# Byte offsets of the weight, activation and feed-forward buffers in a two-layer float32 kernel

## The reference

```
def swiglu(x, w_gate, w_up, w_down):
    return (jax.nn.silu(x @ w_gate) * (x @ w_up)) @ w_down
```

## Time and profile before

| what | before |
|---|---|
| median of 3 runs | 1321.93 us (1321.92 to 1321.98) |
| the profiled execution | 1321.68 us, of which the span of the trace is 1319.9 us |
| PE busy | 1308.6 us, 99% of the span, 7751 matmuls |
| PEld busy | 1105.4 us, 84% |
| DVE, ACT, POOL busy | 1079.1 us (82%), 713.6 us (54%), 205.1 us (16%) |
| share of PE in the chain of work that ended last | 97% |
| granted TensorE clock | 0.999 of full |

### The profile page before, as it was taken

One profiled execution on the slowest core, in us unless ns is written; L12 is line 12 of the kernel. 1 busy time (PEld: TensorE's weight loads), 2 busy tenths in 40 slices (PEclk: granted clock), 3 DMA queues, 4 the chain that ended last, 5 costly groups with the idle time before them and its releaser, 6 DMA issues.

```text
span 1319.9 us, 20183 instructions
## 1 busy us (share of the span) xinstructions
PE 1308.6 (99%) x7751; PEld 1105.4 (84%) x7751; DVE 1079.1 (82%) x1592; ACT 713.6 (54%) x840; POOL 205.1 (16%) x193
## 2 busy tenths in 40 slices
PE   9999999999999999999999999999999999999998
PEld 7888888888888888888899988888888888888886
DVE  6977788868999789998786999769777767878587
ACT  6444455665444454444465688854444466558553
POOL 2400001102000010000000035200000001654940
PEclk9999999999999999999999999999999999999999
DMA  8655556528577654876544565475655555654541
GB/s 274 223 191 191 191 179 204 191 77 306 192 260 267 242 186 146 269 233 222 184 160 155 175 215 180 145 257 166 210 194 196 197 171 160 200 172 143 175 152 56
DMA packets 158445, 254.29 MB, mean 193 GB/s; under 512 B 8800, under 2 KB 99248, under 8 KB 156704
## 3 DMA queue, kind: packets, MB, share of 16 engines
q1 hardware_dynamic: 155136, 232.68, 53.0%
q0 software_dynamic: 2576, 18.45, 4.0%
q10 hardware_dynamic: 656, 2.11, 0.4%
HBM read 252.12 MB, written 1.08 MB: 192 GB/s over the span
## 4 chain that ended last, share of the span: by engine, by line
PE 97%; DVE 1%; issue 1%; ACT 1%; DMA 0%; SPq 0%; POOLq 0%; POOL 0%; DVEq 0%; ACTq 0%
PE psum L718 12%; PE psum L712 12%; PE psum L705 12%; PE psum L736 6%; PE psum L737 5%; PE psum L735 5%; PE psum L2003 4%; PE psum L2004 4%; PE psum L2005 4%; PE psum L438 3%; PE psum L439 3%; PE psum L445 3%; PE psum L473 2%; PE psum L481 2%; PE psum L475 2%; PE psum L504 2%
## 5 line engine op out<-in xcount | busy, mean ns | idle before, releaser
L390 ACT ACTIVATE w_hi<-raw 128x2048 fp32r<-128x2048 f32 (+1 forms) x220 | 419.7, 1910 | 316.5 <-PE psum L718 121.0
L402 DVE TENSOR_TENSOR w_lo<-raw,w_hi 128x2048 fp32r<-128x2048 f32 x219 | 506.8, 2335 | 99.7 <-ACT w_hi L390 98.2
L839 DVE STREAM_TRANSPOSE hidT<-hid 32x128 f32<-32x128 f32 x704 | 213.2, 303 | 22.1
L705 PE MATMUL psum<-w_hi,hT 128*128 128x512 f32 x704 | 174.5, 390 | 0.1
L718 PE MATMUL psum<-w_lo,hT 128*128 128x512 f32 x704 | 173.9, 389 | 0.0
L712 PE MATMUL psum<-w_hi,hT 128*128 128x512 f32 x704 | 173.9, 389 | 0.0
L705 PEld LDWEIGHTS psum<-w_hi,hT 128*128 128x128 f32 x704 | 131.8, 188 | 27.9 <-ACT w_hi L1009 0.8
L712 PEld LDWEIGHTS psum<-w_hi,hT 128*128 128x128 f32 x704 | 132.1, 188 | 27.5
L718 PEld LDWEIGHTS psum<-w_lo,hT 128*128 128x128 f32 x704 | 132.1, 188 | 27.4
L786 ACT ACTIVATE silu_g<-psum,rstd 128x256 f32<-128x256 f32 x88 | 37.0, 472 | 113.5 <-PE psum L718 107.9
L2003 PE MATMUL psum<-w_hi,hT 128*128 128x512 f32 x224 | 88.7, 396 | 0.0
(11 more groups left out here) (407 smaller groups left out, 2180.6 us busy)
## 6 DMA issues: line engine op xcount, KB each, us to landing
raw<-in_ffn_w_down SPq DMA_DIRECT2D x88, 512.0 KB, 5.2
raw<-in_ffn_w_gate SPq DMA_DIRECT2D x87, 512.0 KB, 4.1
raw<-in_ffn_w_up SPq DMA_DIRECT2D x87, 512.0 KB, 5.3
raw<-in_w_in SPq DMA_DIRECT2D x72, 512.0 KB, 4.6
raw<-in_ssm_w_in SPq DMA_DIRECT2D x48, 512.0 KB, 4.6
raw<-in_attn_w_qkv SPq DMA_DIRECT2D x24, 512.0 KB, 4.8
ada_in<-in_w_ada POOLq DMA_DIRECT2D x8, 1536.0 KB, 7.2
raw<-in_ssm_w_out SPq DMA_DIRECT2D x16, 512.0 KB, 4.4
```

What stands on the lines that cost most here:

```text
L390: act.activation(to, src, ACT.Copy).then_inc(sem("hi_ready"), 1)
L402: dve.tensor_tensor(to, src, hi.bitcast(F32), ALU.subtract).then_inc(sem("lo_ready"), 1)
L705: pe.matmul(psum[:, banks[t], :], hT_hi[:, k, t * P:(t + 1) * P], hi[:, kk, :], start=k == 0, stop=False)
L839: dve.transpose(to[:, :, :, 32 * a:32 * (a + 1)], src[:, :, :, 32 * b:32 * (b + 1)])\
```

## The change

The first edit adds 128 bytes in front of `raw`, so that `raw`, `w_hi` and `w_lo` begin at a multiple of 256; another 128 bytes behind `w_lo` bring what follows back to residue 128. Then 64 bytes go in front of `hidT_hi`, and 192 behind `hidT_lo`; and 192 bytes go behind `hidT`, in front of `odd_hidT_hi`. Nothing else is edited. Every later buffer moves by 256 or 512 bytes, which leaves its residue as it was. The engines' lists hold the same instructions in the same order, with other addresses.

```
+        def skip(size):
+            top[0] += size
+
...
         hT = keep("hT", [P, KD, 2, SEQ], R32)
         hT_hi, hT_lo = hT[:, :, 0, :], hT[:, :, 1, :]
+        skip(128)
         raw = keep("raw", [P, SLOTS, UNIT])
         w_hi = keep("w_hi", [P, SLOTS, UNIT], R32)
         w_lo = keep("w_lo", [P, SLOTS, UNIT], R32)
+        skip(128)
         ffn_tiles = top[0]
         silu_g = keep("silu_g", [P, TT, FC])
         hid = keep("hid", [P, TT, FC])
+        skip(64)
         hidT_hi = keep("hidT_hi", [P, 2, SEQ], R32)
         hidT_lo = keep("hidT_lo", [P, 2, SEQ], R32)
+        skip(192)
         const1 = keep("const1", [P, FIRST_W])
...
-        ffn, _ = region(WORK + 7 * 8192)
+        ffn, ffn_end = region(WORK + 7 * 8192)
         hidT = ffn("hidT", [P, 2, SEQ])
+        ffn_end[0] += 192
```

## The result

| what | before | after |
|---|---|---|
| median (lowest to highest, 4 runs each) | 1321.93 us (1321.69 to 1321.98) | 1346.19 us (1345.98 to 1346.47) |
| ratio, 95% interval | | 1.0182 [1.0169, 1.0195] |
| the profiled execution, its span | 1321.68, 1319.9 us | 1346.34, 1344.5 us |

The change costs 24.3 us, 1.8%. It is the price that rival C named for a disturbed pace of all the weight products (1346.7), and it lies above the range.

A forecast was written before the change was run, and what follows sets the result against it. PE, with 97% of the chain, was taken to bound the kernel by starting 7751 matmuls one behind another. Each part of the change was put at 0 us, giving 1321.9 us, with a range of 1271 to 1338.

The forecast's parts named there:

- rival C: Weight products on PE: new distances disturb the even pace, 5.3 ns per matmul, slower, 1325 to 1347 us; chance 0.22.
- The count and the sum: All stages with weights moving: about 4,680 products at 5.3 ns each, 24.8 us more, 1346.7 us.
- the hidden blocks alone: Down products: 1,056 matmuls at the odd distances, disturbed by 5.3 ns each, 5.6 us more, 1327.5 us.
- I take 0 ns per matmul: PE's reads of moving and stationary operands: new starts and distances cost nothing, bounded below by -10.8 ns per matmul.
- the likeliest case: Whole kernel: the addresses do not count, 1321.9 us, own range 1319.3 to 1324.5; chance 0.45.
- The row used against C: Last line 2005 before other work: no load beside it, yet 0.39 us like the others, so loads make no difference.
- the 13.4 ns: Fixed part on top of streaming in every fp32r matmul, at 256 or 512 columns; plain float32 has 2.6 ns.
- five products at 232 ns: Matmuls just behind other work, 1272.88 to 1274.04, before the pace returns; gave the price of 5.3 ns per matmul.
- its two prices: Disturbed pace at 5.3 ns: 1327.5 us on the hidden-layer blocks alone, 1346.7 us on all 4,680 products.
- Rival B: Every fp32r weight product: the fixed part goes, 10.8 ns each, 50.5 us less, 1271 (spread to 1319); chance 0.33.
- some 51 us to give back: Whole kernel: skill's N / 2.4 + 2.5 ns, 215.8 ns at 512 columns against 226.7 measured, leaves about 51 us.
- The rule of the ports: PE's reads: the skill's independent ports for moving operand and weight loads, PE never waiting, so the sum is 0 us.

The follow-up runs named there:

- e3: Kernel before with only the hidden-layer blocks moved, by 64 and 192 bytes, weights left at 128; 1326.95 us, ratio 1.0040.
- e1: Kernel before with every buffer 128 bytes further on, so all starts are multiples of 256 and each product keeps distance 0; 1321.35 us, ratio 0.9997.
- e2: Kernel before with only the weights moved to residue 0, hidden blocks and everything else left at 128; 1346.99 us, ratio 1.0191.
- e9: Kernel before with `hT_lo` alone put 128 bytes off, so only every third product has a distance other than 0; 1330.34 us, ratio 1.0065.
- e4: Kernel before with the weights 64 bytes further on against everything else; 1329.63 us, ratio 1.0060.
- e11: Kernel before with weights 32 bytes further on and line 712's `hT_lo` load halved, leaving out those low-activation products; 1348.17 us, ratio 1.0201.
- e8: Kernel before with the weights 256 bytes further on, hidden blocks kept at distance 0 by another 256; 1321.55 us, ratio 1.0000.
- e5: Kernel before with the weights 32 bytes further on against everything else; 1349.89 us, ratio 1.0214.
- e7: Kernel before with the weights 96 bytes further on against everything else; 1350.11 us, ratio 1.0216.
- e6: Kernel before with the weights 224 bytes further on, distance -32; 1348.87 us, ratio 1.0207.
- e10: Kernel before, distance 0 kept, with line 712's `hT_lo` load halved, leaving out those products for half the tokens; 1326.44 us, ratio 1.0035.

## Why the prediction was wrong, step by step

**What held.** PE's pace is the only way for this change to act: PE's share of the chain is 97% in both kernels, its waits are the same, and the rounding and the remainders on ACT and DVE, which I had costed at 0, did not grow. The count and the sum held too: about 4,680 products with the weights streaming, at 5.3 ns, gave 24.8 us; the measured change of pace is 5.4 ns (232.4 less 227.0) and the loss 24.3 us. For the hidden blocks alone the prediction had 1327.5 us, and `e3` took 1326.95, as the mean of two paces (229.0 ns for the odd blocks and 233.3 for the even ones).

**The step that failed** is "I take 0 ns per matmul", the price of the distance between the two reads. It rested on plain float32 transposes, lines 1210 against 1218 and 1199, which show no effect of start or distance. For the start this was right also in fp32r (`e1`). For the distance it was not: at 128 the 512-column product costs 5 to 6 ns more, as `e1` and `e2` show together, since both have the weights at residue 0 and only `e2` has them at a distance. I had called those rows "weaker evidence for fp32r" and then let them decide the likeliest case.

**The row used against C.** I set, a product without a load beside it and of the same length, against the disturbed pace. That product could tell about distance 0 alone, the only one in that trace. And it was read by its length, whose end is modelled, and to two decimals. From its start to the next, in ns, it speaks for C once other distances are there: 319 before, 325 to 327 after, 330 or 331 in `e9`, without a load beside it in any of them. What it says of the 13.4 ns at distance 0 stays open.

**The row that was right.** The price stood in the earlier trace rows: five products at 232 ns before the pace came back. I read it as a rhythm that loads and streams fall into, and rated the case that they don't at 0.22, with a range that ended halfway between its two prices. It carried the only fp32r evidence for a loss, and should have set the upper end at its full price, 1346.7. That the price fits so closely is in part luck. In ns the five steps are 235, 229, 232, 231 and 227, a mean of 230.8: 4.1 ns and not 5.3, or about 1341 us. At a distance of +64 (`e4`) 1346.7 would have been 17 us too much. And no run shows that products behind other work are slow for the same reason as those at a distance.

**Rival B** falls: with all starts at a multiple of 256 and distance 0 (`e1`) the 13.4 ns stay, and no distance tried brought the mean of the 512-column products below the 227.0 of the kernel before. The Trainium skill, "TensorE: Matmul & The Clock Gate", section "Back-to-back issue gap", has N / 2.4 + 2.5 ns as the gap of a single isolated matmul, an estimate of 215.8 ns at 512 columns; the prediction applied it to a stream and had some 51 us to give back. For a sustained stream of loads and matmuls the same section has about 131 ns at 512 columns. No layout here reached either: 226.7 ns is the best pace of a long group here.

**The rule of the ports.** The Trainium skill, "SBUF — State Buffer", section "Who interferes with whom", has PE's two read ports independent of each other and PE never waiting; by that rule `e2` would cost nothing. It cost 25.3 us with the same instructions in the same order, so for the reads of fp32r products and loads the measurement decides; the ports themselves no run shows.

**What is shown and what stays open.** Shown: the pace depends on the distance modulo 256 of stationary and moving operand; on neither start by itself; 0 is the best of those tried at 512 columns. The same distance gives the same pace from other starts: +64 has 229.0 ns in the odd blocks of `e3`, 229.5 in the even ones of the kernel after and 228.9 in both of `e4`. Line 504, where the weights are stationary and `hT` streams in 512 columns, slowed as well (228.6 to 232.7 ns), so the effect is not bound to the weights being the stream. Not settled: what the two reads share, whether the stream waits for the load or the load for the stream, and why the stream 64 above the load is milder than 64 below. `e9` to `e11` exclude the simple accounts (the beside-load alone, the own operand alone, a cost in proportion to the load) and put none in their place; "rhythm" names what is seen, not a cause.

## What to carry to other kernels

Keep the stationary and the moving fp32r operands of 512-column products at the same residue modulo 256 (0 and 128 were alike); at 256 columns other distances were quicker. A layout that moves one of them by 32 bytes can cost 2% with every wait unchanged. After any change of layout read the time from start to start of one long group, since the busy share stays at 99% either way. A row of another data type bounds a cost only weakly: where the trace holds a few unsettled products of the right type, their pace is the better bound, even if its close fit here was in part luck.

## What was not expected of the hardware

- At 256 columns with `hT` streaming, distance 0 is the slowest: 119.8 ns, against 118.7 at 128, 118.4 at +32, 118.1 at +96, 117.3 at +64 and 116.9 at -32 (means of 889 steps each in `e8`, `e2`, `e5`, `e7`, `e4` and `e6`).
- Products with a half-size load at distance 0 are longer, 230.6 ns in place of 226.7 (`e10`).
- A distance of 256 bytes costs nothing within the measurement, 1.0000 [0.9990, 1.0009], and one of 32 already 1.0214 [1.0197, 1.0232].
- With a distance other than 0 the pace need not settle at one value: of the 2,112 products of gate and up, 2,083 were 226 or 227 ns apart before; after, nearly all are spread over 228 to 241 ns, with none of these values holding more than 332 of them.
